# Hybrid backbone kernel: sums of squares moved ahead of turned tiles, last modulation rows behind the preceding ones, key products shared, state reads one slot ahead

## The reference, cut to what matters

```
qkv = silu(centred_conv(h @ w_in))       # five taps
q, k = l2_normalize(q), l2_normalize(k)  # x * rsqrt(sum(x*x) + eps)
a_mat = strict(k_b @ k.T * decay)        # per chunk and value head
t_inv = inverse(eye + a_mat)
v_new = t_inv @ (v*beta) - t_inv @ (k*beta*exp(g)) @ s
o = (q*exp(g)) @ s + (q @ k.T * decay) @ v_new
s = exp(g_last) * s + k_dec.T @ v_new
```

## Time and profile before

| | |
|---|---|
| median of 3 runs | 2050.78 us (2045.07 to 2051.86) |
| the profiled execution | 2048.42 us |
| its span | 2046.6 us |
| TensorE busy | 1970.7 us, 96% |
| VectorE, ScalarE, GpSimd busy | 714.5, 529.5, 93.1 us |
| mean granted TensorE clock | 0.986 |
| moved by DMA | 193.48 MB, 95 GB/s |

### The profile page before, as it was taken

The page is one execution under the profiler, slowest core; times in us unless marked ns, Lnnn a source line. Parts: engine busy times, 40 slices in busy tenths (PEclk is TensorE's granted clock), DMA queues, the critical chain, the costliest instruction groups (busy, mean ns, idle before and its releaser), DMA issues.

```text
span 2046.6 us, 28698 instructions
## 1 busy us (share of the span) xinstructions
PE 1970.7 (96%) x12112; PEld 1198.9 (59%) x12112; DVE 714.5 (35%) x1476; ACT 529.5 (26%) x1170; POOL 93.1 (5%) x94
## 2 busy tenths in 40 slices
PE   6999999999999999999999999998999998999997
PEld 2444677785654444444444474444776666888886
DVE  2541675105750010000000065555858767010001
ACT  3121325414530020000000042224355776110000
POOL 0000231000000000000000000001211110000000
PEclk9999999999999999999999999999989998999999
DMA  6433111233201212122212132211224101344442
GB/s 280 164 149 126 42 41 42 103 124 125 85 22 62 93 62 82 63 81 82 77 62 72 63 123 67 78 62 63 84 88 183 64 22 43 124 144 144 155 145 91
DMA packets 27997, 193.48 MB, mean 95 GB/s; under 512 B 3004, under 2 KB 4285, under 8 KB 5854
## 3 DMA queue, kind: packets, MB, share of 16 engines
q1 hardware_dynamic: 27826, 191.51, 25.6%
q10 hardware_dynamic: 44, 0.14, 0.0%
HBM read 190.59 MB, written 1.05 MB: 94 GB/s over the span
## 4 chain that ended last, share of the span: by engine, by line
PE 88%; DVE 6%; ACT 3%; issue 1%; DMA 1%; SPq 0%; POOL 0%; ACTq 0%; DVEq 0%; POOLq 0%
PE psum L716 88%; DVE ws_sb L2034 1%; ACT ws_sb L1536 1%; DVE gl_tmp_sb L2034 1%; ACT arena_sb L1536 1%; DVE ws_sb L2037 1%; DMA arena_sb<-w 1%; DVE hT_sb L2037 0%; DVE arena_sb L2043 0%; PE psum L1126 0%; DVE arena_sb L2034 0%; PE psum L975 0%; ACT wide_sb L1536 0%; DVE hT_sb L2034 0%; ACT const_sb L1536 0%
## 5 line engine op out<-in xcount | busy, mean ns | idle before, releaser
L716 PE MATMUL psum<-hT_sb,ring_sb 128*128 128x512 f32 (+2 forms) x2272 | 797.9, 512 | 1.1 <-ACT hT_sb L1536 1.1
L716 PEld LDWEIGHTS psum<-hT_sb,ring_sb 128*128 128x128 f32 (+1 forms) x2272 | 427.9, 189 | 363.2 <-issue 338.6
L716 PE MATMUL psum<-arena_sb,ring_sb 128*128 128x512 f32 (+1 forms) x1216 | 396.2, 487 | 4.2 <-DVE small_sb L2040 1.9
L716 PEld LDWEIGHTS psum<-arena_sb,ring_sb 128*128 128x128 f32 x1216 | 231.5, 191 | 166.2 <-issue 144.0
L1536 ACT ACTIVATE ws_sb<-psum 128x512 f32<-128x512 f32 (+4 forms) x240 | 127.5, 535 | 717.7 <-PE psum L716 707.2
L716 PE MATMUL psum<-ring_sb,hT_sb 128*128 128x256 f32 (+3 forms) x1248 | 240.6, 372 | 0.1
L716 PEld LDWEIGHTS psum<-ring_sb,hT_sb 128*128 128x128 f32 (+1 forms) x1248 | 194.1, 176 | 52.5 <-issue 20.8
L2034 DVE TENSOR_TENSOR arena_sb<-ws_sb,psum 128x512 f32<-128x512 f32 (+1 forms) x44 | 24.4, 554 | 415.1 <-PE psum L716 415.1
L2037 DVE SCALAR_TENSOR_TENSOR xT_sb<-psum,mod_sb,xT_sb 128x256 f32<-128x256 f32 x48 | 23.2, 483 | 387.6 <-PE psum L716 387.1
L2037 DVE SCALAR_TENSOR_TENSOR ws_sb<-ws_sb,cols_sb 128x512 f32<-128x512 f32 (+1 forms) x176 | 123.7, 703 | 6.3
L1536 ACT ACTIVATE wide_sb<-xT_sb 128x512 f32<-128x512 f32 (+1 forms) x40 | 21.8, 544 | 399.8 <-PE psum L716 295.0
(11 more groups left out here) (173 smaller groups left out, 1448.0 us busy)
## 6 DMA issues: line engine op xcount, KB each, us to landing
ring_sb<-w SPq DMA_DIRECT2D x146, 1024.0 KB, 4.8
hT_sb<-w SPq DMA_DIRECT2D x16, 1024.0 KB, 4.9
arena_sb<-w SPq DMA_DIRECT2D x8, 1024.0 KB, 18.9
ring_sb<-w SPq DMA_DIRECT2D x8, 768.0 KB, 4.1
xT_sb<-x SPq DMA_DIRECT2D x1, 2048.0 KB, 10.3
const_sb<-consts SPq DMA_DIRECT2D x1, 2048.0 KB, 9.4
y<-xT_sb SPq DMA_DIRECT2D x1, 1024.0 KB, 4.8
ring_sb<-w SPq DMA_DIRECT2D x2, 256.0 KB, 3.7
```

The lines of the kernel that those rows point to most:

```text
L716: return nc.tensor.matmul(o, l, r, start=start, stop=stop)
```

## The change

Four parts. (1) In `modulation0`, half 7 is issued straight after half 6, ahead of sums 6 and 7, and the `keep_clock(2)` between `columns(2)` and half 7 is gone; the last one stays. (2) In the qkv stage `l2_taken(p)` stands ahead of `evac(t-2)` in VectorE's order, pairs 6 and 7 ahead of the last two `evac`; `l2_scales(0)` is issued at t = 27; the key tiles are scaled three at t = 28, three at 29 and two at 30; `l2_sums(7)` stands ahead of the turned tiles 30 and 31. (3) Items of batch 1 issue no key products: VectorE multiplies with those of batch 0, which now keep a place each (banks 5 and 7, columns 0 and 256). (4) In the loop `reads(i+1)` stands in slot i for i = 3 to 20, `reads(22)` at the end of slot 20; ScalarE does `take(i)` ahead of `read_scaled(i+1)`; the halves of the off-diagonal products stand on either side of `state_steps`.

```diff
+KEYS_SCALED = {28: (0, 1, 2), 29: (3, 4, 5), 30: (6, 7)}
+        def product_bank(n):
+            return (item_banks(n)[1], n % 4 // 2 * 256) if n < 8 else (item_banks(n)[1], 0)
+        def products_of(n):
+            return min(n + 1, 4) if n < 8 else n - 3
# tensor: modulation0
                     rows_half(2 * q)
-                    if q == 0:
-                        rows_half(1)
+                    if q in (0, MOD_FIRST - 1):
+                        rows_half(2 * q + 1)
...
                         columns(q - 1)
-                        if q == MOD_FIRST - 1:
-                            keep_clock(2)
-                        rows_half(2 * q + 1)
+                        if q < MOD_FIRST - 1:
+                            rows_half(2 * q + 1)
# tensor: conv_stage
                 if stage == "qkv":
                     gemm_tok("z1", 0, (2, 3))
+                    l2_sums(7)
# tensor: gdn, item
                     last.then_inc(G["seg"], 1)
+                    if 4 <= n < 8:
+                        return
+                    PB, first = product_bank(n)
...
# tensor: gdn, slots
-                    if 2 <= i < 30:
+                    if 3 <= i <= SUMMED:
+                        reads(i + 1)
+                    elif SUMMED < i < 30:
                         reads(i + 2)
...
-                        off_diagonal_first(OFF_FIRST[i])
+                        off_diagonal_first(OFF_FIRST[i], (0,))
-                        off_diagonal_second(OFF_SECOND[i])
+                        off_diagonal_second(OFF_SECOND[i], (0,))
...
                     if i < 28:
                         state_steps(i)
+                    if i in OFF_FIRST:
+                        off_diagonal_first(OFF_FIRST[i], (1,))
+                    if i in OFF_SECOND:
+                        off_diagonal_second(OFF_SECOND[i], (1,))
                     if 15 <= i < 31:
                         query_reads(i + 1)
+                    if i == SUMMED:
+                        reads(i + 2)
# scalar
-                    if stage == "qkv" and t == 29:
+                    if stage == "qkv" and t == 27:
                         l2_scales(0)
...
                 for i in range(32):
+                    take(i)
                     if 3 <= i < SUMMED - 1:
                         read_scaled(i + 1)
-                    take(i)
# vector: conv_stage, after conv t
+                    if stage == "qkv" and t >= 20 and t % 2 == 0:
+                        l2_taken(t // 2 - 10)
+                    if stage == "qkv" and t in (28, 30):
+                        l2_scaled(KEYS_SCALED[t])
                     if t >= 2:
                         evac(t - 2)
+                    if stage == "qkv" and t == 29:
+                        l2_scaled(KEYS_SCALED[t])
...
-                    if stage == "qkv" and t >= 20 and t % 2 == 0:
-                        l2_taken(t // 2 - 10)
-                    if stage == "qkv" and t == 31:
-                        dve.wait_ge(S["l2_rs"], 1)
-                        l2_scaled(0)
...
+                if stage == "qkv":
+                    l2_taken(6)
+                    l2_taken(7)
                 evac(info["tiles"] - 2)
                 evac(info["tiles"] - 1)
# vector: gdn, item
-                    dve.wait_ge(G["kk"], n + 1)
+                    dve.wait_ge(G["kk"], products_of(n))
```

More of the change, by code:

```diff
@@ L1279, in item @@
                     j = 2 * s + t // 2
-                    PA, PB = item_banks(n)
+                    PA = item_banks(n)[0]
                     dec = wide[:, n % 2, :].rearrange("p (u y) -> p u y", y=64)
@@ L1312, in item @@
                                 other = k1[:, hq, at + 32 * (1 - i % 2):at + 32 * (1 - i % 2) + 32]
-                                mm(psum[32 * i:32 * i + 32, PB, 32 * q:32 * q + 32], own_toks, own_toks)
-                                last = mm(psum[32 * i:32 * i + 32, PB, 128 + 32 * q:160 + 32 * q], own_toks, other)
+                                mm(psum[32 * i:32 * i + 32, PB, first + 32 * q:first + 32 * q + 32], own_toks, own_toks)
+                                last = mm(psum[32 * i:32 * i + 32, PB, first + 128 + 32 * q:first + 160 + 32 * q], own_toks, other)
                         else:
@@ L1326, in off_diagonal_first @@
                     base_t = bases(b)[1]
-                    for hf in range(2):
+                    for hf in halves_of:
                         for u in range(16):
@@ L1333, in off_diagonal_first, with off_diagonal_second @@
                         last.then_inc(G["z"], 1)
-                def off_diagonal_second(b):
+                def off_diagonal_second(b, halves_of=(0, 1)):
                     s, ty, e0 = batch(b)
                     base_r = bases(b)[0]
-                    for hf in range(2):
+                    for hf in halves_of:
                         pe.wait_ge(G["z_copied"], 2 * b + hf + 1)
@@ L1517, in _ @@
             conv_stage("qkv")
-            l2_sums(7)
             gdn()
@@ L2085, in norm, with l2_scaled @@
                         own(stt(h, x, gain[:, i, which, c, s:s + 1], r, ALU.mult, ALU.mult).then_inc(S["scaled"], 1), S["scaled"])
-            def l2_scaled(p):
-                for i in range(p, p + 8):
+            def l2_scaled(tiles):
+                dve.wait_ge(S["l2_rs"], 1)
+                for i in tiles:
                     a = l2_src(i)
@@ L2358, in item @@
                     n, t = item_no(b, nl), nl % 4
-                    PB = item_banks(n)[1]
+                    PB, first = product_bank(n)
                     dve.wait_ge(G["exp"], n + 1)
-                    dve.wait_ge(G["kk"], n + 1)
+                    dve.wait_ge(G["kk"], products_of(n))
                     if nl < 4:
                         u = u_flat(b)[:, 512 * t:512 * t + 512].rearrange("p (x v c) -> p x v c", v=2, c=32)
-                        ins = tt(u, u, bc(psum[:, PB, 0:256].rearrange("p (x c) -> p x c", c=32), 2, 2), ALU.mult)
+                        ins = tt(u, u, bc(psum[:, PB, first:first + 256].rearrange("p (x c) -> p x c", c=32), 2, 2), ALU.mult)
                     else:
@@ L2540, in _ @@
             conv_stage("qkv")
-            for p in (6, 7):
-                l2_taken(p)
             gdn()
```

4 lines of the change are left out of this document (2 added, 2 removed).

## The result

| | kernel before | changed kernel |
|---|---|---|
| median of the runs | 2049.45 us (2045.07 to 2051.86, 4 runs) | 2027.61 us (2027.17 to 2033.33, 4 runs) |
| ratio | | 0.9907 (0.9893 to 0.9922) |
| profiled execution, its span | 2048.42, 2046.6 us | 2033.33, 2031.5 us |
| mean granted clock | 0.986 | 0.986 (0.989 to 0.990 in the other three) |

What follows compares the result with a forecast made beforehand. TensorE was taken as the bound (88% of the chain), with VectorE where it ends last. Terms 3.2 + 9.4 + 3.1 + 4.5 = 20.2 us off 2048.4 gave 2028.2, forecast as 2029 us; range 2021 to 2040.

Steps and rivals of the forecast that it cites:

- Modulation, 3.2: Start of kernel: filler 1.9, a 0.78 wait and 0.58 idle go ahead of the first GEMM, saving 3.2 us.
- the bound of 32.5: Modulation: half 7's last block, issued at about 7.5 and at most 25.0 us to landing, lands no later than 32.5.
- Sums of squares, 9.4: qkv stage: four boundary waits go (4.9), then 0.3, 1.6 at pair 5 and 2.6 up to the first item; 9.4 us.
- Shared products, 3.1: Items of batch 1: without their key products VectorE's last product comes earlier, saving 3.1 us.
- What VectorE does afterwards (53.5 us) is unchanged: Behind batch 1's last product: VectorE's remaining 53.5 us stay the same and TensorE keeps waiting some 3.5 us.
- The other value that I gave, 1.5: Shared products: 1.5 us remains if the two idles of 0.65 and 0.94 us meet the exponents too.
- The loop, 4.5: Loop slots: waits 2.7 and clock 3.1 gained, less 0.8 at outputs(17) and 0.5 at slot 19; 4.5 us.
- I count it as gone: Slot 15: the fallen clock behind the 1.93 us idle, which cost 3.1 us, no longer occurs.
- 0, and 3.1 if it doesn't: Slot 20: the clock falls again with 2.0 us idle, gaining 0; 3.1 us if it stays up.
- The clock at 1424,: First items: 2.3 us of idle remain, so the clock stays fallen, gaining 0; up to 1.7 us otherwise.
- The clock that takes part of it back: Rival: slow clock in slot 15 and modulation, and items' idles, take back 8 of 20 us; 2037 us, chance 0.25.
- The scaled copy is hidden: Loop: take and scaled copy (2.4 us) hide behind 4.1 us of TensorE work; rival of exposure: 2068 us, chance 0.03.

Runs made afterwards that it cites:

- sums as before: Changed kernel with the qkv stage's sums of squares, scales and key scaling put back as in the kernel before: 2042.71 us, ratio 0.9967.
- changed again: The changed kernel measured and profiled a second time, unaltered, against the kernel before: 2028.95 us, ratio 0.9905.

## Why the prediction was right, and where not

**The total** was right: 2029 against 2027.6, inside the range. Part of that is luck. The stage's end and boundaries gave 1.1 more than worked out, the shared products 1.9 less, and the loop's figure mixes two values, neither of them the forecast's. Undone one by one the parts cost 2.9, 10.5 (at equal clock), 1.2 and 4.8, together 19.4; the median of the changed kernel's eight runs lies 20.2 below the 2048.39 of the kernel before in the repetition. The terms, against what undoing each part shows:

*Modulation, 3.2.* 2.9 by the medians, 2.7 to 3.5 by the profiles. The block of half 7 landed at 32.49, inside the bound of 32.5, but half 6 was done by 32.0 in that execution, and half 7 waited 0.47. In the profile taken again it did not wait, and the stretch from the sums of q = 2 to the first GEMM is 12.0 us (29.01 to 41.02) where it was 15.5 (28.30 to 43.83). The clock didn't fall in the first GEMM.

*Sums of squares, 9.4.* 10.5 at equal clock; the first two profiles show the same (110.05 us from the sums of pair 0 to the first item, 120.56 before), and the 9.9 of the run's expectation was too low. From sums(2) to sums(3) it takes 16.33 us and took 17.79, so a boundary gave 1.46 and not its wait of 1.23. The copies of pair 4 are waited for 0.94 and not 0.7. The end is as worked out: 1.7 for 1.6 at pair 5, and 2.6 from there to the first item. What was short is the price of a boundary, since work without the wait in it also runs a little faster (four sums in 1.88 us, before 1.96).

*Shared products, 3.1.* 1.2 by the run without them, 1.5 between the two first profiles. The failing step is "What VectorE does afterwards (53.5 us) is unchanged". It takes 55.0, since GpSimd's scalings, which the key products had covered, then ran beside the elimination. The last product did come 3.0 us nearer to `to_lanes(0)` (from 15.43 to 12.45). The other value that I gave, 1.5, is closer, but by another road: with the products kept, one idle time of 0.37 us with no releaser stands in batch 1, where the earlier trace rows has 0.65 and 0.94, so these idles are not bound to the products. Nor were they simply spared: in the changed kernel two of 0.67 and 0.96 us stand in batch 0, which had one of 0.19 before.

*The loop, 4.5.* 4.8 by the medians; 5.8 or 1.3 by the profile. The waits of slots 13 and 15 went (2.7), `outputs(19)` waits 1.98 as worked out, and `outputs(17)` doesn't wait, so that 0.8 was too much. The step that failed here is "I count it as gone": slot 15's clock still fell in 11 of the 12 profiles with the new order of reads, for 3.4 us and not 6.8, behind a wait of 0.82 us for `mod1_copy` that the forecast doesn't have, and those 3.4 us cost 2.1. The clock in slot 20, "0, and 3.1 if it doesn't" fall, is the term with two values: the same kernel runs with it and without, at 4.5 us. So the medians' 4.8 lies between 5.8 and 1.3, and meets the forecast's 4.5 by luck.

*The clock at 1424,* kept fallen at 0: the size was right, the fall wasn't. In both profiles of the changed kernel the clock stayed up at the first items, and the 1.7 us that the forecast had for that case didn't come: C is 77.07 us with a fall of 6.8 us there (sums as before) and 77.07 without (changed again).

*Rivals.* The clock that takes part of it back is real, but in GLA and slot 20, and in some executions only. I had argued from the length of the idle times in one profile; that the same wait is followed by a fall in half of the executions could not be read there. The scaled copy is hidden, as expected. Still open: what decides the clock in GLA and in slot 20, where the idle times without a releaser come from, and what the halves are worth.

## What to carry to other kernels

Work that is taken out of one engine moves all that follows it against the others: ask what ran beside the removed instructions and what it will run beside now, above all GpSimd instructions beside VectorE's two-operand ones. When one kernel's executions differ by more than the effect looked for, compare distances between the same events at equal clock, and let repeated profiles tell what belongs to the change. A wait that was predicted and could have been removed is worth removing: here it gave back 2.0 us in the loop, and the slow clock that followed it in half of the executions was not seen again in four profiles.

## What the hardware showed that I had not expected

VectorE's elimination steps, both inputs in SBUF, doubled from 0.38 to 0.78 us beside GpSimd's multiplies (one step at their side kept its 0.36), while products with a PSUM input (0.69), 32x32 transposes (2.0) and steps beside a GpSimd memset (0.39) did not change. The price of a stretch at 1.2 GHz depends on what runs in it: 10.2 us cost 4.5 in slots 20 and 21, 3.4 us cost 2.1 in slot 15 (D 175.02 and 172.89, otherwise the same loop), 13.7 us cost 4.7 in GLA, and 6.8 us at the first items (sums as before) cost nothing that can be told from the idle times without a releaser there: 9.56 us to `to_lanes(0)`, against 9.47 in a profile without the fall (changed again). The last may come from VectorE ending last behind them; that is argued and not shown.
